# Norm statistics split from their table functions, weight slabs of the first units placed between modulation slabs, and a new hand-written order in a three-block fp32 kernel

## The reference

```python
mod = jax.nn.silu(c) @ w_ada[l] + b_ada[l]
sh1, sc1, g1, sh2, sc2, g2 = jnp.split(mod[:, None, :], 6, axis=-1)
hn = (_rms(x, norm1_g[l]) * (1 + sc1) + sh1).astype(x.dtype)
y = _mixer(hn, w_in[l], ...)
x = x + g1 * (y.astype(x.dtype) @ w_out[l])
hn = (_rms(x, norm2_g[l]) * (1 + sc2) + sh2).astype(x.dtype)
gate, up = jnp.split(hn @ w_gate_up[l], 2, axis=-1)
x = x + g2 * ((jax.nn.silu(gate) * up) @ w_down[l])
```

## Time and profile before

| | |
|---|---|
| median of 3 runs | 1057.93 us (1055.76 to 1059.59) |
| profiled execution | 1057.78 us, span 1056.0 us |
| TensorE busy | 1022.9 us, 97% |
| VectorE busy | 752.0 us, 71% |
| ScalarE busy | 537.2 us, 51% |
| mean granted clock of TensorE | 0.994 of full |
| read from HBM | 179.04 MB, 171 GB/s |

### The profile page before, as it was taken

One profiled execution on the slowest core, in us unless ns is written; L12 is line 12 of the kernel. 1 busy time (PEld: TensorE's weight loads), 2 busy tenths in 40 slices (PEclk: granted clock), 3 DMA queues, 4 the chain that ended last, 5 costly groups with the idle time before them and its releaser, 6 DMA issues.

```text
span 1056.0 us, 21568 instructions
## 1 busy us (share of the span) xinstructions
PE 1022.9 (97%) x9120; PEld 898.4 (85%) x9120; DVE 752.0 (71%) x1049; ACT 537.2 (51%) x597; POOL 0.5 (0%) x7
## 2 busy tenths in 40 slices
PE   9999999999989999999999999989999989999998
PEld 7999999999866798989898787659976759999986
DVE  5999956778458658777787866867887674565544
ACT  5665454474263464445646433776687463334431
POOL 0000000000000000000000000000000000000000
PEclk8999999999999999999999999999999999999999
DMA  8454342244416664325443544884453364555441
GB/s 350 161 182 160 124 157 94 108 160 160 161 41 254 238 240 167 141 93 191 144 138 122 191 165 177 326 336 173 141 179 121 120 239 160 206 193 178 162 170 49
DMA packets 26302, 181.47 MB, mean 172 GB/s; under 512 B 3040, under 2 KB 3296, under 8 KB 4960
## 3 DMA queue, kind: packets, MB, share of 16 engines
q1 hardware_dynamic: 25056, 174.66, 45.2%
q10 hardware_dynamic: 1152, 5.45, 1.3%
HBM read 179.04 MB, written 1.05 MB: 171 GB/s over the span
## 4 chain that ended last, share of the span: by engine, by line
PE 88%; DVE 6%; ACT 3%; issue 1%; DMA 1%; ACTq 0%; SPq 0%; DVEq 0%
PE PS L910 85%; PE PS L1073 1%; ACT WH L1380 1%; DVE WL L1791 1%; PE PS L1151 1%; DMA layer<-xt 1%; DVE X L1988 1%; DVE X L1987 1%; PE PS L1301 1%; DVE STAT L1969 0%; DVE X L1968 0%; PE PS L1190 0%; DVE layer_ln L2101 0%; DVE layer L2094 0%; PE PS L1000 0%
## 5 line engine op out<-in xcount | busy, mean ns | idle before, releaser
L910 PE MATMUL PS<-XTH,WH 128*128 128x256 f32 x1392 | 403.7, 290 | 5.3 <-issue 1.6
L910 PE MATMUL PS<-XTL,WH 128*128 128x256 f32 x1392 | 394.8, 284 | 0.0
L910 PE MATMUL PS<-XTH,WL 128*128 128x256 f32 x1392 | 394.7, 284 | 0.0
L1791 DVE TENSOR_TENSOR WL<-RAW,WH 128x2048 fp32r<-128x2048 f32 x138 | 314.2, 2277 | 107.4 <-ACT WH L1380 104.2
L1380 ACT ACTIVATE WH<-RAW 128x2048 fp32r<-128x2048 f32 x138 | 262.7, 1903 | 217.0 <-PE PS L910 213.5
L910 PEld LDWEIGHTS PS<-XTH,WH 128*128 128x128 f32 x1392 | 267.8, 192 | 10.2 <-issue 4.0
L910 PEld LDWEIGHTS PS<-XTL,WH 128*128 128x128 f32 x1392 | 268.1, 193 | 2.1 <-issue 1.9
L910 PEld LDWEIGHTS PS<-XTH,WL 128*128 128x128 f32 x1392 | 267.8, 192 | 0.0
L910 PE MATMUL PS<-WH,YH 128*128 128x512 f32 x224 | 89.7, 400 | 1.1 <-DVE YL L2266 1.1
L910 PE MATMUL PS<-WH,YL 128*128 128x512 f32 x224 | 87.3, 390 | 0.0
L910 PE MATMUL PS<-WL,YH 128*128 128x512 f32 x224 | 87.3, 390 | 0.0
(11 more groups left out here) (293 smaller groups left out, 1116.9 us busy)
## 6 DMA issues: line engine op xcount, KB each, us to landing
RAW<-wst SPq DMA_DIRECT2D x162, 1024.0 KB, 4.9
LNW<-lnrow ACTq DMA_DIRECT2D x3, 1024.0 KB, 8.2
RAW<-wst SPq DMA_DIRECT2D x4, 512.0 KB, 4.8
layer<-xt SPq DMA_DIRECT2D x2, 512.0 KB, 5.3
XR<-x ACTq DMA_DIRECT2D x1, 1024.0 KB, 4.7
out<-X SPq DMA_DIRECT2D x4, 256.0 KB, 2.3
CST<-cst ACTq DMA_DIRECT2D x1, 640.0 KB, 8.6
PT<-pt SPq DMA_DIRECT2D x1, 512.0 KB, 5.6
```

The costliest lines, as they stand in the source:

```text
L910: return pe.matmul(o, lhsT, rhs, start=start, stop=stop)
L1791: tt(WL[:, i % RAW_RING, 0:n], RAW[:, i % RAW_RING, 0:n], as_float(WH[:, k % SPLIT_RING, 0:n]), ALU.subtract).then_inc(vector_done, 1)
```

## The change

The three steps of the norm become: `rms:i:c:n`, the square alone, in no set of functions; `rma:i`, one scaling of both tiles' first sums; `rmt:i:c`, the `Ln` and `Exp`. VectorE's `rmsb` waits for `rmt`.

```diff
-          "natural_log_exp_and_others": ("ba1", "ba2", "gc", "norm", "gr", "lna", "lb", "hr", "rms", "qn", "ga",
+          "natural_log_exp_and_others": ("ba1", "ba2", "gc", "norm", "gr", "lna", "lb", "hr", "rma", "rmt", "qn", "ga",
...
         for c in range(NT):
             for n in range(2):
                 step("rms", i, c, n, on="S")
+            if c == 0:
+                step("rma", i, on="S")
+            step("rmt", i, c, on="S")
             step("rmsb", i, c, on="V")
...
-                link(fn(XN[:, c, s], X[:, c, s], ACT.Square, accum_out=SUMSQ[:, c, n:n + 1]))
-                if n == 0:
-                    fn(SUMA[:, c:c + 1], SUMSQ[:, c, 0:1], ACT.Identity, scale=1.0 / D, bias=EPS[:, 1:2]).then_inc(scalar_done, 1)
-                    return
+                fn(XN[:, c, s], X[:, c, s], ACT.Square, accum_out=SUMSQ[:, c, n:n + 1]).then_inc(scalar_done, 1)
+
+            def s_rma(i):
+                fn(SUMA[:], SUMSQ[:, :, 0], ACT.Identity, scale=1.0 / D, bias=EPS[:, 1:2]).then_inc(scalar_done, 1)
+
+            def s_rmt(i, c):
```

```diff
     rms(0)
+    loaded_before(("ada", 9, 0), ("feat", 8))
     ada(9)[0]()
...
     rms(1)
+    loaded_before(("ada", 10, 0), ("ff", 0), ("ada", 10, 1), ("ff", 1))
     ada(10)[0]()
```

The order tables are written anew. Some fifty places differ on TensorE, most by a neighbour or two; one row of the table at the second entry shows the kind:

```diff
-first:out2:0:1 out2:0:1 first:out2:1:1 out2:1:1 ada:10:0 xt:5:2 ada:10:1 ada:11:0 xt:5:0 xt:5:3 xt:5:1
+first:out2:0:1 first:out2:1:1 out2:0:1 out2:1:1 ada:10:0 ada:10:1 ada:11:0 adat:10 xt:5:0 xt:5:1 xt:5:2 xt:5:3
```

More of the change, by code:

```diff
@@ L485 @@
[L485 to L489, removed]
+gu:1:3:0 gp:1:3:1 gx:1:2:1 gx:1:3:0 gp:1:4:0 gu:1:3:1 gu:1:4:0 gp:1:4:1 gx:1:3:1 gx:1:4:0 gp:1:5:0 gu:1:4:1 gu:1:5:0
@@ L508 @@
-adat:10 ada:11:1 adat:11 ff:1 ff:0 ff:2 ff:3 ff:5 ff:4 ff:6 ff:8 ff:7 ff:9 ff:11 ff:10 ff:12 ff:13 ff:14 ff:15 ff:16
-ff:17 ff:18 ff:19 ff:20 ff:21 down:0:0 down:0:1 down:0:2 down:0:3 down:0:4 first:down:0:5 down:1:0 down:0:5 down:1:1
+gate:1:0:1 first:gate:1:1:0 adat:6 first:gate:1:1:1 gate:1:1:0 gate:1:1:1 ada:7:0 ada:7:1 ada:9:0 ada:9:1 ada:4:0
+adat:7 xt:4:1 xt:4:0 xt:4:2 xt:4:3 adat:9 ada:4:1 first:feat:8 gates:0 feat:8 gates:1 first:feat:0 qn:1:2 gcol feat:0
+first:feat:1 qn:0:0 feat:1 grow:0 first:feat:2 qn:0:1 grow:1 feat:2 first:feat:3 qn:0:2 grow:2 feat:3 first:feat:4
@@ new lines @@
+split:26:26 gv:0:1 gq:0:0 split:27:27 gr:0:0 split:28:28 az:1:0 zb:1:0 split:29:29 gc:1 zb:1:1 c1 split:30:30 norm:q:1
+split:31:31 split:32:32 ah:1:1 split:33:33 az:1:1 split:34:34 split:35:35 gx:1:1:0 split:36:36 gx:1:1:1 gx:1:2:0
+gx:1:2:1 gx:1:3:0 xl gx:1:3:1 gx:1:4:0 gx:1:4:1 gx:1:5:0 gx:1:5:1 gv:1:0 gs:1 split:38:38 split:37:37 lb gv:1:1
+split:39:39 gq:1:0 gq:1:1 gr:1:0 gr:1:1 pl:0:0 lna:0:0 xt:0:0:0 lna:0:1 pl:0:1 split:40:45 xt:0:0:1 ada:0:1 xt:0:1:0
+split:41:46 ada:1:1 split:42:47 xt:0:1:1 first:gate:0:0:1 split:43:48 gate:0:0:1 first:gate:0:1:1 split:44:51 xt:1:0
@@ new lines @@
+hc:2 q1:3:0 hq:2:0 split:74:81 q1:3:1 hr:2:0 split:75:82 split:76:85 i:3:1 split:77:86 z1:3:0 z1:3:1 split:78:87
+ada:3:1 split:79:88 split:80:89 hc:3 split:81:90 hq:3:1 hq:3:0 hr:3:0 split:82:91 hr:3:1 split:83:92 pl:1:0 lna:1:0
+lna:1:1 xt:2:0:0 pl:1:1 xt:2:0:1 split:84:98 xt:2:1:0 ada:8:1 split:85:99 ada:6:1 split:86:100 xt:2:1:1
+first:gate:1:0:1 rms:0:0:0 split:87:101 gate:1:0:1 first:gate:1:1:1 split:88:105 rms:0:1:0 rms:0:0:1 gate:1:1:1 rma:0
+rmt:0:0 rms:0:1:1 rmt:0:1 ada:7:1 ada:9:1 xt:4:0 xt:4:1 xt:4:2 xt:4:3 split:89:109 ada:4:1 feat:8 ga gb split:90:110
@@ L566 @@
-hp:2:5 hp:2:6 hy:2:7 f:3:0 split:73:80 split:72:79 hz:2 split:74:81 hy:3:0 hd:3 hy:3:1 hr:2:0 hp:3:0 hy:3:2
-split:75:82 hy:3:3 hp:3:1 split:76:85 hy:3:4 hp:3:2 hp:3:3 hy:3:5 hy:3:6 hp:3:5 hp:3:4 adat:3 split:77:86 hp:3:6
-split:78:87 hy:3:7 split:79:88 mod:0 split:80:89 hz:3 split:81:90 split:82:91 hr:3:0 split:83:92 hr:3:1
-first:out:1:1:3 first:out:1:0:3 lna:1:0 lnb:1:0:0 out:1:0:3 out:1:1:3 lna:1:1 lnb:1:0:1 lnb:1:1:0 lnb:1:1:1
-split:84:98 xt:2:0:0 split:85:99 xt:2:0:1 adat:8 xt:2:1:1 xt:2:1:0 wg2 first:gate:1:0:1 split:86:100 split:87:101
@@ new lines @@
+gc:1 split:29:29 vtr:1 gc2:1 split:30:30 norm:q:1 gk:1 split:31:31 ac:1:1 gkk:1 split:32:32 ab:1:1 gp:1:0:1 gp:1:0:0
+split:33:33 gu:1:0:0 gu:1:0:1 split:34:34 gp:1:1:0 gp:1:1:1 gu:1:1:0 gp:1:2:0 split:35:35 gu:1:1:1 split:36:36
+gu:1:2:0 wg gp:1:2:1 gp:1:3:0 gu:1:2:1 gu:1:3:0 gp:1:3:1 gp:1:4:0 gu:1:3:1 gu:1:4:0 gp:1:4:1 gp:1:5:0 gu:1:4:1
+gu:1:5:0 gp:1:5:1 gp:1:6:0 gu:1:5:1 gu:1:6:0 gp:1:6:1 split:38:38 gu:1:6:1 gks:1 lb split:39:39 split:37:37 gz:1
+gr:1:0 gr:1:1 first:out:0:0:3 c1 first:out:0:1:3 lna:0:0 lnb:0:0:0 out:0:0:3 out:0:1:3 xt:0:0:0 lna:0:1 lnb:0:0:1
@@ new lines @@
+split:79:88 split:81:90 split:80:89 hz:3 hr:3:0 split:82:91 split:83:92 hr:3:1 first:out:1:1:3 first:out:1:0:3 lna:1:0
+lnb:1:0:0 out:1:0:3 out:1:1:3 lna:1:1 lnb:1:0:1 lnb:1:1:0 lnb:1:1:1 split:84:98 xt:2:0:0 xt:2:0:1 split:85:99 adat:8
+xt:2:1:0 split:86:100 mod:0 xt:2:1:1 first:gate:1:0:1 split:87:101 adat:6 first:gate:1:1:1 gate:1:0:1 split:88:105
+gate:1:1:1 wg2 rmsb:0:0 rmsb:0:1 adat:7 xt:4:1 xt:4:3 xtl:4:0 xtl:4:1 adat:9 xtl:4:2 xtl:4:3 gates:0 split:89:109
+gates:1 ga gb gd split:90:110 qn:1:2 gcol split:91:111 mb:2 mb:1 qn:0:0 grow:0 split:92:112 grow:1 qn:0:1 split:93:113
@@ L585 @@
+split:131:157 ff:20 split:132:158 ff:21 split:133:159 first:down:0:5 split:134:160 down:0:5 split:135:161
+split:136:162 split:137:163 split:138:164 first:down:1:5 down:1:5
 """
```

160 lines of the change are left out of this document (73 added, 87 removed).

## The result

| | before | after |
|---|---|---|
| median of the runs | 1056.85 us (4 runs) | 1050.23 us (1047.82 to 1050.46, 4 runs) |
| ratio to before | | 0.9933, interval 0.9918 to 0.9947 |
| profiled execution, span | 1057.78, 1056.0 us | 1050.20, 1048.4 us |
| TensorE busy | 1022.9 us | 1019.6 us |
| table loads on line 1726 (1734 after) | 41 | 36 |

The change makes the kernel faster by 7.1 us (5.6 to 8.7). The forecast was 4.5. A second job gave the change 0.9933 again (0.9919 to 0.9946); one of its five executions there ran at a mean clock of 0.654 for 1413.89 us and is in no ratio, and the median of the other four is 1049.86 us.

A forecast was written before the change was run, and what follows sets the result against it. TensorE, busy 1022.9 of 1056.0 us, was taken as the bound. Terms -3.6 + 0 + 0 - 1.0 + 0.1 = -4.5 us against 1057.78 us gave 1053.3 us; own range 1051.5 to 1055.3, 8-in-10 range 1050.0 to 1057.8.

The forecast's parts named there:

- The rest: Some fifty swaps of neighbouring steps, each covering a wait and opening one of the same size: +0.1 us, bounds -1.5 and +1.5.
- the first entry: Near 700 us: TensorE idles for slab 107, time given back by later steps; norm split counted 0: 0 us, bounds ±2.5.
- gkk:0: First delta rule: its 1.00 us wait for gk:0 on VectorE goes: -1.0 us, bounds 0 and -1.2.
- the second entry: After the last output product, near 850 us: ada products and adat fill the normed-tile wait: chain -3.8 us, taken -3.6.
- its clock term: Second entry: granted clock 0.61 of full from 854 to 858 us, counted in part only through shorter products.
- The clock stays up: Rival: half-clock stretches vanish at both entries and small swaps give 1.0 us: gain 7, 1050.8 us; chance 0.15.
- The base: Starting time for the sum: profiled execution of before, 1057.78 us, taken as 0.15 us under the median of the runs.
- The gain was not handed on: Rival: slabs 134 and 111, asked for later, land late and hand the gain on: 1056.6 us, no change; chance 0.25.
- no queue starved: Rival: slabs asked for in bursts land in 13.7 us, delaying feat:2 and ff:3: slower, 1064.0 us; chance 0.08.

The follow-up runs named there:

- early: Kernel before with the changed order of all three engines up to the last gate of the first block, the rest as before: ratio 0.9983 to before.
- no_second: The change with the second entry in the order of before and its slabs in their old places, norm still split: ratio 0.9987 to before.
- gk_only: Kernel before with gk:0 alone moved, on TensorE ahead of v:1:0 and on VectorE ahead of gc2:0: ratio 0.9999 to before.
- gk_set: Kernel before with the changed order of all engines up to gp:0:0:1: ratio 0.9995 to before.
- chain_end: Kernel before with the end of the second delta chain alone in the changed order, out:0:1:1 moved late: ratio 1.0006 to before.
- chain_wg: chain_end with VectorE's long steps wg and setup moved ahead as well: ratio 0.9990 to before.
- late: The change with the order of before up to the last gate of the first block: ratio 0.9950 to before.
- no_first: The change with the first entry in the order of before, feat:8 in slab 108, norm still split: ratio 0.9958 to before.
- no_split: The change's slabs and orders with the unsplit norm of before: ratio 0.9921 to before, median 1048.35 us.
- lnw_early: The change with the 1 MB DMA of the norm rows issued behind the gate's first half: ratios 0.9906 and, in a second job, 0.9904 to before.
- lnw_no_split: lnw_early with the unsplit norm of before and its table loads: ratio 0.9916 to before, median 1048.01 us.
- slab_swap: lnw_early with slabs 130 and 131 exchanged and the split of ff:1 behind the modulation on ScalarE: ratio 0.9923 to before.
- warm_change: The change with three products of constants while TensorE waits for slab 107: ratio 0.9933 to before, median 1049.19 us.
- combined: lnw_early with attention's order of before and one filler product each at 12 us and ahead of the fifth ada product: ratio 0.9918 to before.

## Why the prediction was right and wrong

The sum was too small, 4.5 us against 7.1, and the measured 1050.23 us lies below the forecast's own range of 1051.5 to 1055.3. The step that failed is "The rest" (+0.1), with its "each covers a wait and opens one of the same size": the small swaps bring 1.1 us net by the traces, half of what the traces gain over the forecast once the stall at 546 us is set aside. With the start of the kernel and the stall taken out, the traces of `early` and of the change are both 2.5 us ahead at the first entry, of which `gkk:0` is 1.24. The times point the same way without deciding it: `early` gained 1.8 us (0.8 to 2.6) where the prediction's terms give 0.9. The other half is spread: the second entry 0.35 us more, the first 0.6, `gkk:0` 0.24. By time the second entry gives more still, since its clock term was priced from one trace. Each term follows.

The rival "The clock stays up" named 1050.8 us, nearest to the measured time, but by luck: the stretch at the first entry that it counts as gone is still there, and the small swaps give what it adds.

**The second entry (taken -3.6, chain -3.8): right, and in its parts.** By its slabs the trace shows -3.95. The chain put the transposes at 856.2 and `ff:0` at 859.2 us; the measured starts, 852.30 and 855.58, with the 3.66 us of lead added, are 855.96 and 859.24.

**The clock's part of the second entry: a term that was too small.** I took one step lost at the second entry from the one trace of before. Seven traces with the old order there (before, `early`, `no_second`, `gk_only`, `gk_set`, `chain_end`, `chain_wg`) show one step three times and two steps four times, 2.7 us on the mean; the ten traces with the new order there and its slabs, in `slab_swap` with two of them exchanged (the change, `late`, `no_first`, `no_split`, `lnw_early` twice, `lnw_no_split`, `slab_swap`, `warm_change`, `combined`) show none at the second entry. So on the mean 0.57 of a step more goes away than I counted, at 1.2 to 1.4 us each some 0.7 us (an estimate), and `late` measured 5.3 us where the two traces give 4.4; its interval does not resolve the difference. Filling idle time alone is worth 1.6 us to the kernel before.

**The first entry (0, measured -0.6): near in sum, by luck in part.** The wait for slab 107 was the right mechanism. It landed after 6.4 us, not 7.7. What was wrong inside the term is the norm's split, "with slab 107 later than either, I count 0": with the scaling, `Ln` and `Exp` behind the sigmoid the DMA of the norm rows leaves sooner, and that DMA is what makes slab 107 late. By time the effect, 1.3 us, is not resolved. The same MB moved 18 us ahead is worth 3 us. I had seen both transfers in the earlier trace rows and took their collision as given.

**`gkk:0` (-1.0): right in the change, -1.24,** though alone 0.75 of it would have been given back, by the trace of `gk_only`.

**"The rest" (+0.1, bounds -1.5 and +1.5): wrong, the step that failed.** The trace shows -0.3 by 128 us, -0.8 at the end of the second chain and -0.1 at 344; with +0.15 in attention it is -1.1, inside the bounds. The reasoning "each covers a wait and opens one of the same size" holds for a swap made alone, as `chain_end` and `gk_only` show. The table moves them in groups, and in the two groups that I took apart the second member removes the wait that the first one opens. I weighed them one by one.

**The base.** The profiled execution of before, 1057.78 us, lies 1.2 us above the median of 21 further runs (1056.6 us); I had set it equal to the median of three. The stall at 546 us is part of that.

**Rivals.** The gain was not handed on and no queue starved. Slab 111 was asked for at 713.8 and slab 134 at 861.9 us, within 0.7 us of the forecast less the lead, and the first of each burst landed as fast as a slab that is alone:

```profile
RAW<-wst SPq DMA_DIRECT2D x1, 1024.0 KB, 4.7
```

for slab 111, and 5.0 us for slab 134. The Trainium skill, page "DMA: Bandwidth & Descriptors", section "Queues, rings and completion order", says that each engine takes a queue's descriptors in ring order, and the trace agrees: the first of four slabs asked for together takes 4.7, the fourth 12.0 us. Against the same skill's "ScalarE: Activation LUTs", section "What ACT_TABLE_LOAD costs", this trace again shows no drain:

```profile
692.15 1.28 ACT L1734 ACT_TABLE_LOAD   x1
693.45 0.29 ACT L1628 ACTIVATE SUMA<-SUMSQ,EPS 128x2 f32<-128x2 f32 x1
```

## What to carry to other kernels

Fill a wait with work whose weights are already on chip, and see that these weights are split in time too: with the splits behind the modulation the new order cost here all that it had brought. A transfer of another queue that starts in the same moment as the one you wait for is worth a look before anything else (moving it brought 3 us here, more than any other single edit behind the change), and what delays or advances its issue (three small activations, here) belongs into the sum. Judge swaps in a hand-written order in groups, by asking which wait the partner removes. Take a term that depends on the clock from several executions, and before you read a wait from a trace, see whether its execution is like the others in time.

## What was unexpected of the hardware

The clock's loss behind an idle stretch came in equal portions, 1.7 us each, zero, one or two of them for the same order of work. The kernel before shows it in its times: of 91 runs, the 13 with a mean clock of 0.996 took 1055.1 us on the mean, the 39 with 0.993 took 1057.1.

TensorE stalls labelled "issue", up to 0.8 us long, stand in runs of 32-wide products at 546 us in some executions and not in others of the same order, with 0.27, 0.54 or 0.82 us (0.27 in the change, at 542.98). No run here shows their cause.
